# K projection of six token tiles as one level of Strassen over head pairs, its weight operands streamed from memory

## The chip, the cores and the metric

One Trainium2 chip, all 8 NeuronCores (two dies of four). Every core runs the same program on its own 2,048 tokens and recomputes keys and values for the 2,048 tokens ahead of them, so no core talks to another. The metric is the device time in microseconds of the slowest core for one execution of the whole layer.

## The reference, cut to what matters

One decoder layer: a combined projection, two groups of attention heads (group A dilated, group B a sliding window), `w_out`, LayerNorm, SwiGLU, LayerNorm. The change touches the projection of group A's keys and, lightly, the rotary tables of the queries.

```python
proj = jnp.einsum('bsd,de->bse', x, w_in) + b_in          # d = 2048
qa, ka, va, qb, kb, vb = jnp.split(proj, cuts, axis=-1)   # ka: 8 heads x 128
ka = rope(ka.reshape(B, S, 8, 128), pos)                  # [x1*cos - x2*sin, x2*cos + x1*sin]
...
qa = rope(qa.reshape(B, S, 8, 128), pos); qb, kb = rope(...)   # heads of 64 in group B
```

## The kernel before

The program has three phases: phase 1 projects K and V of all 4,096 tokens of a core, phase 2 projects the queries and does the attention, phase 3 does `w_out`, the norms and the feed-forward layer (itself in Strassen form, most of the span). The change lies in phase 1, with a small piece in phase 2.

Phase 1 holds the tokens as x tiles 0 to 7 of 512 tokens: `xs[slot]` is [128, 16 chunks of the contraction, 512 tokens], cast from float32 to bf16 by the load. Tiles 0 and 1 open the program (V by quarters of the contraction, while the weights still arrive). Then each tile t runs:

- two **V units** (`v_unit`, from tile 2 on), one level of Strassen over contraction halves, token halves and column halves: seven products "4 5 1 2 3 7 6" of eight matmuls, on four PSUM banks A, B, Dk, C. Products 1, 2, 5, 6, 7 read sums of x (`xp`, `xq`, `xr`) which `x_sum(t, 0..2)` makes on VectorE during the tile before. Product "7" adds into bank A and can start only when VectorE has read A into `v4`;
- from tile 3 on one **kb tile** and one **vb tile**, the small projections for group B;
- eight **K tiles** (`k_tile(t, h)`, h = head): 16 matmuls of 512 columns with the resident weights `wk[h]`, then the rotation `rope_a(..., swap=True)`: two ScalarE copies of 64 partitions that swap the halves, then three VectorE operations, then a store to `ka` in memory. `nx("bk", 8)` hands the eight PSUM banks out in turn.

The order of work is that in which the Python code calls the helpers; every engine runs its own instructions strictly in that order. `Sched` derives the semaphore waits from named buffers and byte ranges: a buffer laid over an older one waits for all the readers of the older one. A DMA is an instruction of its queue's engine: `"pool"` (needed for the casting loads), `"sp"` or `"act"`. The DMA waits for its buffers in that engine's order, so what is behind it in the queue waits too.

Phase 2 begins with `phase2_loads` in tile 7: three query weights on the pool queue (`wq`), the group B tables `rb` on the ScalarE queue. The group A tables `ra` come in one load of 2,048 KB in unit u = 3 of 32. `proj(tau)` is a query tile; tau 0 to 31 use `rb`, tau 32 to 63 use `ra`, and unit u runs `proj(u + 6)`.

The softmax here doesn't subtract the row's maximum and nothing guards it: scores larger than these inputs give would overflow.

## Time and profile before

| | us |
|---|---|
| median of 3 runs | 2787.43 |
| the runs | 2787.43, 3201.25, 2781.75 |
| profiled execution, span of the slowest core | 2774.6 |
| TensorE busy in it | 2720.6 |
| K projection units of tiles 2 to 7 (six of 27.6) | 166 |

The span runs from the first to the last instruction of the core. Of the profiled execution only this span is given; the two lower runs lie 7.2 and 12.8 us above it, which is what lies around a span. The run of 3201.25 us is disturbed and is left out of comparisons. Times inside the profile are counted from the span's start, and a stretch is named by them (tile 4's K units are 207.6 to 235.2).

### The profile page before, as it was taken

How to read it: one execution, taken by the hardware profiler on the slowest of the kernel's cores; microseconds unless marked ns; L12 is line 12 of the kernel's file. 1: busy time of each engine (PE TensorE's matmuls, PEld its weight loads, DVE VectorE, ACT ScalarE, POOL GpSimd, SP SyncE). 2: the span in 40 equal slices, each digit the busy share in tenths (PEclk: the TensorE clock that was granted, in tenths of full speed). 3: DMA queues.
4: the chain of work that ended last, by engine and by line, in shares of the span. 5: the costliest groups of instructions: out<-in, count | busy, mean ns of one | idle time of the engine just before them, and what ended most of it. 6: DMA issues, size and time to landing. Idle time of an engine off the chain costs nothing.

```text
span 2774.6 us, 41975 instructions; the slowest of 8 cores (2770.5 to 2774.6 us)
## 1 busy us (share of the span) xinstructions
PE 2720.6 (98%) x14991; PEld 1297.4 (47%) x14991; DVE 1990.6 (72%) x2758; ACT 843.0 (30%) x1229; POOL 569.9 (21%) x588
## 2 busy tenths in 40 slices
PE   8999999999999999999999999999999999999995
PEld 3444444445666444444444444444444444444442
DVE  4866665898888736788866666666988765766767
ACT  0312222787667237333200122111333100212115
POOL 3100000232112557311100101056000000000165
PEclk9999999999999999999999999999999999999998
DMA  9953135567567648789989776788799798555734
GB/s 153 193 118 87 48 86 134 114 130 150 129 149 188 198 144 250 124 154 157 149 169 211 135 122 114 129 227 212 164 171 167 144 194 188 85 83 90 174 115 122
DMA packets 254159, 407.23 MB, mean 147 GB/s; under 512 B 91969, under 2 KB 129985, under 8 KB 253378
## 3 DMA queue, kind: packets, MB, share of 16 engines
q0 software_dynamic: 92336, 193.64, 44.7%
q1 hardware_dynamic: 146066, 179.44, 21.7%
q10 hardware_dynamic: 15552, 31.46, 3.5%
q8 instruction: 122, 2.00, 0.3%
q14 instruction: 83, 0.68, 0.1%
HBM read 490.84 MB, written 104.27 MB: 214 GB/s over the span
## 4 chain that ended last, share of the span: by engine, by line
PE 91%; DMA 3%; DVE 3%; issue 1%; ACT 1%; POOL 0%; DVEq 0%; ACTq 0%; POOLq 0%; SPq 0%
PE sp L1570 57%; PE sp L902 8%; PE sp L1376 8%; PE sp L640 6%; PE sp L576 5%; DMA arena<-xT 3%; PE sp L1094 1%; PE sp L522 1%; PE sp L1112 1%; PE sp L945 1%; PE sp L971 1%; PE sp L620 1%; PE sp L661 1%; PE sp L1036 1%; PE sp L987 0%
## 5 line engine op out<-in xcount | busy, mean ns | idle before, releaser
L1570 PE MATMUL sp<-arena 128*128 128x512 f16 x7408 | 1600.0, 379 | 0.0
L1570 PEld LDWEIGHTS sp<-arena 128*128 128x128 f16 (+1 forms) x7408 | 724.7, 98 | 875.7 <-issue 3.1
L1844 DVE TENSOR_TENSOR arena<-sp,arena 128x512 f32<-128x512 f32 (+1 forms) x348 | 236.6, 689 | 161.0 <-PE sp L1570 141.9
L1930 DVE TENSOR_TENSOR arena<-arena,sp 128x512 f32<-128x512 f32 x257 | 169.9, 683 | 147.5 <-PE sp L1570 147.2
L902 PE MATMUL sp<-arena 128*128 128x512 bf16 x1024 | 236.8, 379 | 3.0 <-DVE arena L356 3.0
L140 POOL DMA_DIRECT2D arena<-wup x88 | 66.7, 758 | 771.8 <-DVE arena L1583 461.3
L1376 PE MATMUL sp<-arena 128*128 128x512 bf16 x1024 | 221.8, 379 | 2.2 <-DVE arena L1365 2.2
L640 PE MATMUL sp<-arena 128*128 128x512 bf16 x1024 | 222.2, 379 | 0.0
L1878 ACT ACTIVATE arena<-sp 128x512 f32<-128x512 f32 x86 | 51.4, 597 | 416.9 <-PE sp L1570 416.9
L363 ACT ACTIVATE arena<-sp,arena 64x512 f32<-64x512 f32 x136 | 92.9, 683 | 273.1 <-PE sp L640 247.4
L1419 POOL TENSOR_TENSOR arena<-arena 128x512 f32<-128x512 f32 x117 | 149.4, 1278 | 112.9 <-DVE arena L1930 74.0
L1418 ACT ACTIVATE arena<-arena 128x512 f32<-128x512 f32 x117 | 73.7, 630 | 283.3 <-DVE arena L1930 136.7
L1591 DVE TENSOR_TENSOR arena<-arena 128x2048 f16<-128x2048 bf16 (+1 forms) x118 | 159.4, 1351 | 0.0
L1376 PEld LDWEIGHTS sp<-arena 128*128 128x128 bf16 x1024 | 100.1, 98 | 124.2 <-issue 4.6
L1583 DVE TENSOR_TENSOR arena<-arena 128x2048 f16<-128x2048 bf16 (+1 forms) x118 | 157.3, 1333 | 0.0
L640 PEld LDWEIGHTS sp<-arena 128*128 128x128 bf16 x1024 | 100.0, 98 | 119.7
L1844 DVE TENSOR_TENSOR arena<-arena 128x512 f16<-128x512 f32 (+1 forms) x304 | 154.9, 568 | 0.3 <-issue 0.3
L1421 POOL TENSOR_TENSOR arena<-arena 128x512 f32<-128x512 f32 x117 | 151.1, 1292 | 9.2 <-ACT arena L1418 8.2
L902 PEld LDWEIGHTS sp<-arena 128*128 128x128 bf16 x1024 | 95.5, 98 | 120.7 <-issue 12.2
L576 PE MATMUL sp<-arena 128*128 128x512 f16 (+1 forms) x672 | 147.9, 379 | 1.6 <-DVE arena L586 1.6
L1841 ACT ACTIVATE arena<-sp 128x512 f32<-128x512 f32 x90 | 53.5, 597 | 277.8 <-PE sp L1570 248.8
L1053 ACT ACTIVATE arena<-sp 128x1024 bf16<-128x1024 f32 x96 | 97.4, 1020 | 68.2 <-PE sp L1047 56.4
(153 smaller groups left out, 2602.3 us busy)
## 6 DMA issues: line engine op xcount, KB each, us to landing
arena<-wup POOLq DMA_DIRECT2D x88, 1024.0 KB, 11.3
arena<-wdn POOLq DMA_DIRECT2D x22, 1408.0 KB, 16.5
z2s<-arena SPq DMA_DIRECT2D x39, 512.0 KB, 12.8
arena<-wob SPq DMA_DIRECT2D x32, 512.0 KB, 4.9
arena<-xres SPq DMA_DIRECT2D x32, 512.0 KB, 5.9
x1s<-arena ACTq DMA_DIRECT2D x64, 256.0 KB, 5.3
arena<-z2s SPq DMA_DIRECT2D x29, 512.0 KB, 12.3
arena<-wdb POOLq DMA_DIRECT2D x10, 1408.0 KB, 11.0
```

The costliest lines, as they stand in the source:

```text
L576: ins = nc.tensor.matmul(bank(k, bk), w[:, c, :], m[:, c, :], start=(first and c == 0), stop=(last and c == 7), skip_group_check=True)
L640: ins = nc.tensor.matmul(bank(k, bk), wk[h][:, kc, :], x[:, kc, :], start=(kc == 0), stop=(kc == KC - 1))
L902: ins = nc.tensor.matmul(bank(k, bk), w[:, kc, :], x[:, kc, :], start=(kc == 0), stop=(kc == KC - 1))
L1053: S_.act(lambda: nc.scalar.activation(out=p, in_=sp[:, :], func=AF.Exp, scale=scA), spb[s], [bp])
L1376: ins = nc.tensor.matmul(bank(k, bk), w[:, kc, :], y[:, kc, hh * 512:(hh + 1) * 512], start=(first and i == 0), stop=(last and i == len(kc ...
L1419: S_.pool(lambda: nc.gpsimd.tensor_tensor(out=za, in0=za, in1=z, op=ALU.add), [bz, bza], [bza])
L1421: ss["pend"] = [lambda: S_.pool(lambda: nc.gpsimd.tensor_tensor(out=qa, in0=qa, in1=sq, op=ALU.add), [bsq, bqa], [bqa])]
L1570: ins = nc.tensor.matmul(bank(k, bk), w, x, start=(first and i == 0), stop=(last and i == len(ws) - 1), skip_group_check=True)
L1583: S_.dve(lambda: nc.vector.tensor_tensor(out=v, in0=w[:, 0:n, :], in1=w[:, n:2 * n, :], op=ALU.add), [bw], [b])
L1591: S_.dve(lambda: nc.vector.tensor_tensor(out=v, in0=w[:, :, 0:128], in1=w[:, :, 128:256], op=ALU.subtract), [bw], [b])
L1844: S_.dve(lambda: nc.vector.tensor_tensor(out=o, in0=a, in1=b, op=op), [ba, bb], [bo])
L1930: S_.dve(lambda: nc.vector.tensor_tensor(out=v, in0=v, in1=o, op=op), [b, bo], [b])
```

## The change

For x tiles 2 to 7 the eight `k_tile`s are replaced by four `k_pair(t, p, mids)`. A pair takes heads 2p and 2p+1, the two halves of the contraction and the two 256-token halves, and forms the four output blocks from seven products of eight matmuls of 256 columns: 224 matmuls a tile where there were 128 of 512 columns. Its moving operands are the x sums that the V units already have. Its stationary operands are seven blocks for each pair, five of them sums of weights:

- `k_sums(p)` makes them on VectorE: three sums into a scratch of three buffers `kg`, two in place in `wk`. Seven stores of 256 KB on SyncE's queue put all seven into a new array `kwc` in memory. Pairs 0 to 2 are done inside tile 1 (behind `k_tile(1, 3)`, `(1, 5)`, `(1, 7)`), pair 3 behind the first V unit of tile 2.
- `k_load(t, p)` brings the seven blocks back, in two DMAs (1,024 and 768 KB) on the pool queue, into one of two places over the old `wk`. Pair p of a tile ends with the load for the pair after the next.

The results of the products are combined by two or three ScalarE copies and five VectorE operations of 256 columns a pair, and the rotation then works from memory-side float32 tiles (`ca`, `cb`): per head the two half copies on ScalarE and three VectorE operations of 512 columns. The rotations of a pair run inside the next pair (`mids`); those of pair 3 run inside the first V unit of the next tile (`settled`). The three x sums for the next tile all move to pair 3. The vb tile moves ahead of the V units, `load_x`, `load_ta` and `load_tb` to the new places. In phase 2 `rb` becomes four buffers and moves onto what was `wv`/`wkb`, and `ra` is loaded over it in four pieces behind units 23 to 26.

```diff
+    k.kwc_d = dt("kwc", [4, 128, 7, 1024], BF16, kind="Internal").ap()
...
+    OPS = "4512376"
...
+    def k_sums(p):
+        blk = lambda h, i: wk[h][:, 8 * i:8 * i + 8, :]
+        h0, h1 = 2 * p, 2 * p + 1
+        gs = []
+        for i, (a, b_, op) in enumerate((((h0, 1), (h0, 0), ALU.subtract), ((h0, 0), (h1, 1), ALU.add), ((h1, 0), (h1, 1), ALU.subtract))):
+            o_ = o_kg + 2048 * i
+            v, b = view(k, o_, 1024, F16).rearrange("p (a b) -> p a b", a=8), S_.buf("kg%d_%d" % (p, i), o_, o_ + 2048)
+            S_.dve(lambda v=v, a=a, b_=b_, op=op: nc.vector.tensor_tensor(out=v, in0=blk(*a), in1=blk(*b_), op=op), [bwk[h0], bwk[h1]], [b])
+            gs.append((o_, b))
+        for d, o in (((h0, 1), (h1, 1)), ((h1, 0), (h0, 0))):
+            S_.dve(lambda d=d, o=o: nc.vector.tensor_tensor(out=blk(*d).bitcast(F16), in0=blk(*d), in1=blk(*o), op=ALU.add),
+                   [bwk[h0], bwk[h1]], [bwk[d[0]]])
+        src = {"4": gs[0], "1": gs[1], "3": gs[2], "2": (o_k + 4096 * h0, bwk[h0]), "7": (o_k + 4096 * h0 + 2048, bwk[h0]),
+               "6": (o_k + 4096 * h1, bwk[h1]), "5": (o_k + 4096 * h1 + 2048, bwk[h1])}
+        bw = []
+        for i, n in enumerate(OPS):
+            o_, b_ = src[n]
+            b = Buf("kwc%d_%d" % (p, i))
+            S_.dma("sp", k.kwc_d[p, :, i, :], view(k, o_, 1024), [b_], [b], "kwc")
+            bw.append(b)
+        k.bkwc[p] = bw
+
+    def k_load(t, p):
+        if t > 7:
+            return
+        o_ = o_k + 4096 + 14336 * (p % 2)
+        for a, e in ((0, 4), (4, 7)):
+            b = S_.buf("kw%d_%d_%d" % (t, p, a), o_ + 2048 * a, o_ + 2048 * e)
+            S_.dma("pool", view(k, o_ + 2048 * a, 1024 * (e - a)), k.kwc_d[p, :, a:e, :].rearrange("p a n -> p (a n)"), k.bkwc[p][a:e], [b], "kw")
+            for i in range(a, e):
+                v = view(k, o_ + 2048 * i, 1024, BF16 if OPS[i] in "25" else F16).rearrange("p (a b) -> p a b", a=8)
+                KW[t, p, OPS[i]] = (v, b)
...
+    def k_pair(t, p, mids):
...
+        A, B, Dk, C = [nx("bk", 8) for _ in range(4)]
+        lo, up = slice(0, 256), slice(256, 512)
+        W = {"4": (x[:, 8:16, up], bxt), "3": (x[:, 0:8, lo], bxt), "1": (xq3, [bxq]), "5": (xp3[:, :, lo], [bxp]),
+             "2": (xp3[:, :, up], [bxp]), "7": (xr3[:, 8:16], [bxr]), "6": (xr3[:, 0:8], [bxr])}
+
+        def prod(n, bk, first, last):
+            (w, bw), (m, bm) = KW[t, p, n], W[n]
...
+            def mm():
+                for c in range(8):
+                    ins = nc.tensor.matmul(bank(k, bk)[:, 0:256], w[:, c, :], m[:, c, :], start=(first and c == 0), stop=(last and c == 7),
+                                           skip_group_check=True)
+                return ins
+            S_.pe(mm, [bw] + bm, [k.bBK[bk]])
...
+        prod("4", A, True, True)
+        S_.act(lambda: nc.scalar.activation(out=v4, in_=ps[A], func=AF.Identity, bias=bias(h0), scale=1.0), [bb[A], k.bsmall], [b4])
+        mid()
+        prod("5", B, True, True)
+        S_.act(lambda: nc.scalar.activation(out=v5, in_=ps[B], func=AF.Copy), [bb[B]], [b5])
+        prod("1", Dk, True, True)
+        S_.dve(lambda: nc.vector.tensor_tensor(out=v5, in0=ps[Dk], in1=v5, op=ALU.subtract), [bb[Dk], b5], [b5])
+        prod("2", C, True, True)
+        S_.dve(lambda: nc.vector.tensor_tensor(out=ca[:, up], in0=ps[C], in1=v4, op=ALU.add), [bb[C], b4], [bca])
+        mid()
+        prod("3", B, False, True)
+        S_.act(lambda: nc.scalar.activation(out=cb[:, lo], in_=ps[B], func=AF.Identity, bias=bias(h1), scale=1.0), [bb[B], k.bsmall], [bcb])
+        prod("7", A, False, True)
+        S_.dve(lambda: nc.vector.scalar_tensor_tensor(out=ca[:, lo], in0=ps[A], scalar=bias(h0), in1=v5, op0=ALU.add, op1=ALU.add),
+               [bb[A], b5, k.bsmall], [], [bca])
+        prod("6", C, False, True)
+        k_load(t if p < 2 else t + 1, (p + 2) % 4)
+        S_.dve(lambda: nc.vector.tensor_tensor(out=v5, in0=v5, in1=ps[C], op=ALU.subtract), [bb[C], b5], [b5])
+        S_.dve(lambda: nc.vector.scalar_tensor_tensor(out=cb[:, up], in0=ps[B], scalar=bias(h1), in1=v5, op0=ALU.add, op1=ALU.add),
+               [bb[B], b5, k.bsmall], [], [bcb])
+        mid()
...
+        def rope(h, c, bc):
...
+            for i, j in ((0, 64), (64, 0)):
+                S_.act(lambda i=i, j=j: nc.scalar.activation(out=t2[i:i + 64], in_=c[j:j + 64], func=AF.Copy), [bc], [bt2] if i == 0 else [],
+                       [bt2] if i else [])
+            ko, bko = KO[ki := nx("ko", 5 if t < 6 else 3)]
+            S_.dve(lambda: nc.vector.tensor_tensor(out=c, in0=c, in1=ra[:, 0, :], op=ALU.mult), [bc, bra], [bc])
+            S_.dve(lambda: nc.vector.tensor_tensor(out=t2, in0=t2, in1=ra[:, 1, :], op=ALU.mult), [bt2, bra], [bt2])
+            S_.dve(lambda: nc.vector.tensor_tensor(out=ko, in0=c, in1=t2, op=ALU.add), [bc, bt2], [bko])
...
+        return [lambda: rope(h0, ca, bca), lambda: rope(h1, cb, bcb)]
...
+    for h in range(8):
+        k_tile(1, h)
+        if h in (2, 4, 6):
+            x_sum(2, h // 2 - 1)
+        if h in (3, 5, 7):
+            k_sums(h // 2 - 1)
+    k_temps()
+    k_load(2, 0)
+    load_x(4, (8, 8))
+    load_ta(3)
...
+    def settled(t):
+        while ropes:
+            ropes.pop(0)()
...
+        if t == 5:
+            load_x(7, (8, 8))
...
+    for t in range(2, 8):
+        if t >= 3:
+            vb_tile(t)
+        v_unit(t, 0, lambda: settled(t - 1))
+        if t == 2:
+            k_sums(3)
+            k_load(2, 1)
+        if t >= 3:
+            kb_tile(t)
...
-        for h in range(8):
-            k_tile(t, h)
-            xi = {2: 0, 4: 1, 6: 2} if t == 1 else {1: 0, 3: 1, 5: 2}
-            if h in xi and t < 7:
-                x_sum(t + 1, xi[h])
...
+        for p in range(4):
+            mids = ropes + [lambda: None] * (2 - len(ropes))
+            if p == 3 and t < 7:
+                r = mids.pop(1)
+                mids += [lambda: (x_sum(t + 1, 0), x_sum(t + 1, 1)), lambda: (x_sum(t + 1, 2), r())]
+            ropes = k_pair(t, p, mids)
+            if t == 7 and p == 1:
                 phase2_late(k)
...
+    k.o_ra = P.o
+    k.rb = [P("rb%d" % t, 1024, F32) for t in range(4)]
...
     for t in range(4):
-        S_.dma("act", k.rb[:, t], k.ropeB_d[t], [], [], "rbq", joins=[k.brb])
+        S_.dma("act", k.rb[t][0], k.ropeB_d[t], [], [k.rb[t][1]], "rbq")
...
-        S_.dma("sp", ra, k.ropeA_d[4:8].rearrange("t p a b -> p t a b"), [], [bra], "raq")
...
+    def load_ra(t):
+        o = o_ra + t * 4096
+        v, b = view(k, o, 1024, F32), S_.buf("raq%d" % t, o, o + 4096)
+        S_.dma("sp", v, k.ropeA_d[4 + t], [], [b], "raq")
+        ra.append((v.rearrange("p (a b) -> p a b", a=2), b))
...
+        if 23 <= u < 27:
+            load_ra(u - 23)
```

Where the instructions stand now, at three places.

VectorE at the end of tile 1, from the rotation of `k_tile(1, 6)` to the first read of a V unit's bank A (L586 before, L589 after), before:

```order
L356 SCALAR_TENSOR_TENSOR arena<-sp,arena 128x512 [waits e_act]
L366 TENSOR_TENSOR arena<-arena 128x512
L359 TENSOR_TENSOR arena<-arena 128x512 [waits e_dve,d_56]
L556 TENSOR_TENSOR arena<-arena 128x4096 [waits d_52,d_51,d_5]
L356 SCALAR_TENSOR_TENSOR arena<-sp,arena 128x512 [waits e_act]
L366 TENSOR_TENSOR arena<-arena 128x512
L359 TENSOR_TENSOR arena<-arena 128x512 [waits e_dve,d_57]
L586 TENSOR_TENSOR arena<-sp,arena 128x512 [waits e_pe]
```

and after (L357/L367/L360 are the rotation, L559 is `x_sum`, L626 and L629 are `k_sums`):

```order
L357 SCALAR_TENSOR_TENSOR arena<-sp,arena 128x512 [waits e_act]
L367 TENSOR_TENSOR arena<-arena 128x512
L360 TENSOR_TENSOR arena<-arena 128x512 [waits e_dve,d_56]
L559 TENSOR_TENSOR arena<-arena 128x4096 [waits d_52,d_51,d_5]
L357 SCALAR_TENSOR_TENSOR arena<-sp,arena 128x512 [waits e_act]
L367 TENSOR_TENSOR arena<-arena 128x512
L360 TENSOR_TENSOR arena<-arena 128x512 [waits e_dve,d_57]
L626 TENSOR_TENSOR arena<-arena 128x1024 [waits d_2]
L626 TENSOR_TENSOR arena<-arena 128x1024 [waits d_60]
L626 TENSOR_TENSOR arena<-arena 128x1024 [waits d_64]
L629 TENSOR_TENSOR arena<-arena 128x1024 [waits e_dve] x2
L589 TENSOR_TENSOR arena<-sp,arena 128x512 [waits e_pe]
```

The five weight sums of pair 2 now stand ahead of the V unit's first read; those of pairs 0 and 1 stand likewise behind heads 3 and 5. The waits `d_...` of L626 are for stores that still read `kg`.

The pool queue from the load of x tile 3 on, before:

```order
L140 DMA arena<-xT 128x8x512 [waits e_pe]
L140 DMA arena<-xT 128x8x512
L140 DMA arena<-xT 128x8x512 [waits e_pe]
L140 DMA arena<-xT 128x8x512 [waits d_53,d_52,d_51,d_5,d_4,d_3,d_2,d_1,d_0]
```

and after (128x4096 and 128x3072 are the two parts of a `k_load`; the first two x rows are tile 3, the next two tile 4):

```order
L140 DMA arena<-xT 128x8x512 [waits e_pe]
L140 DMA arena<-xT 128x8x512
L140 DMA arena<-kwc 128x4096 [waits d_65,d_63,d_62,d_54,d_3]
L140 DMA arena<-kwc 128x3072 [waits d_64,d_2,d_66,d_4,d_61]
L140 DMA arena<-xT 128x8x512
L140 DMA arena<-xT 128x8x512 [waits d_1,d_0]
L140 DMA arena<-kwc 128x4096 [waits d_71,d_69,d_67,d_52]
L140 DMA arena<-kwc 128x3072 [waits d_72,d_57]
L140 DMA arena<-kwc 128x4096 [waits e_pe]
```

The load of tile 4 now stands behind `k_load(2, 0)`, whose waits `d_...` are stores of `kwc`, and `k_load(2, 1)` stands behind the load of tile 4.

SyncE's queue in the first half of phase 2, before:

```order
L140 DMA ys<-arena 128x2048 [waits e_dve]
L140 DMA arena<-ropeA 128x4x1024
L140 DMA ys<-arena 128x2048 [waits e_dve] x4
L140 DMA arena<-ka 128x8x512 [waits d_56,d_0,d_5]
L140 DMA arena<-vs 128x17x128
L140 DMA arena<-vs 128x5x128 x4
L140 DMA arena<-vs 128x16x128 x2
```

and after:

```order
L140 DMA ys<-arena 128x2048 [waits e_dve] x5
L140 DMA arena<-ka 128x8x512 [waits d_50,d_58,d_1]
L140 DMA arena<-vs 128x17x128
L140 DMA arena<-vs 128x5x128 x4
L140 DMA arena<-vs 128x16x128 x2
L140 DMA ys<-arena 128x2048 [waits e_dve]
L140 DMA arena<-ropeA 128x1024 [waits e_dve] x4
L140 DMA ys<-arena 128x2048 [waits e_dve] x2
```

The tables `ra` moved from ahead of the loads of head 0's keys and values (`ka`, `vs`) to behind them.

## Rows read from the trace of the kernel before

**Rows 1.** The page, parts 1 and 4: busy time, chain that ended last.
```profile
PE 2720.6 (98%) x14991; PEld 1297.4 (47%) x14991; DVE 1990.6 (72%) x2758; ACT 843.0 (30%) x1229; POOL 569.9 (21%) x588
...
PE 91%; DMA 3%; DVE 3%; issue 1%; ACT 1%; POOL 0%; DVEq 0%; ACTq 0%; POOLq 0%; SPq 0%
PE sp L1570 57%; PE sp L902 8%; PE sp L1376 8%; PE sp L640 6%; PE sp L576 5%; DMA arena<-xT 3%; PE sp L1094 1%; PE sp L522 1%; PE sp L1112 1%; PE sp L945 1%; PE sp L971 1%; PE sp L620 1%; PE sp L661 1%; PE sp L1036 1%; PE sp L987 0%
```

**Rows 2.** Spans and clock: die 1, whose median core is the longer.
```profile
die 1 (median of its cores): 2772.5 us, clock 0.996
```

**Rows 3.** TensorE timeline: start us, us, line, shape, count, idle before.
```profile
127.83 8.80 PE L576 MATMUL sp<-arena 128*128 128x512 f16 x40
137.71 13.97 PE L576 MATMUL sp<-arena 128*128 128x512 f16 x64 [1.09 <-DVE arena L586]
...
207.60 27.79 PE L640 MATMUL sp<-arena 128*128 128x512 bf16 x128
...
263.07 3.74 PE L620 MATMUL sp<-arena 128*128 128x128 bf16 x64
```

**Rows 4.** Windows of tile 4's K units and of tile 5's V/kb/vb units.
```profile
207.60:235.20 27.60, 27.60 (x131) 12.53 (x129) 20.02 (x27) 9.56 (x14) 0.00 (x0) 1.00 0.12 40
235.20:266.60 31.40, 31.40 (x194) 16.15 (x193) 17.57 (x26) 3.25 (x5) 1.75 (x2) 1.00 0.72 140
```

**Rows 5.** VectorE timeline at the end of tile 1.
```profile
120.71 2.29 DVE L556 TENSOR_TENSOR arena<-arena 128x4096 f16<-128x4096 bf16 x1 [4.80 <-DMA arena<-xT]
122.92 0.74 DVE L356 SCALAR_TENSOR_TENSOR arena<-sp,arena 128x512 f32<-128x512 f32 x1
...
125.04 0.74 DVE L356 SCALAR_TENSOR_TENSOR arena<-sp,arena 128x512 f32<-128x512 f32 x1
...
127.17 1.22 DVE L556 TENSOR_TENSOR arena<-arena 128x2048 f16<-128x2048 bf16 x1
...
136.88 1.28 DVE L586 TENSOR_TENSOR arena<-sp,arena 128x512 f32<-128x512 f32 x2
```

**Rows 6.** VectorE timeline, a 128-wide operation on PSUM.
```profile
196.69 0.29 DVE L392 TENSOR_TENSOR arena<-sp,arena 128x128 f32<-128x128 f32 x1 [0.26 <-PE sp L389]
```

**Rows 7.** ScalarE timeline, the half copies of one K unit.
```profile
157.73 1.38 ACT L363 ACTIVATE arena<-sp,arena 64x512 f32<-64x512 f32 x2 [12.20 <-PE sp L640]
```

**Rows 8.** DMA issues of 60 to 77 us: KB each, us to landing.
```profile
vs<-arena SPq DMA_DIRECT2D x8, 256.0 KB, 19.5
```

**Rows 9.** DMA issues of 300 to 360 us.
```profile
arena<-xT POOLq DMA_DIRECT2D x2, 1024.0 KB, 18.3
vs<-arena SPq DMA_DIRECT2D x4, 256.0 KB, 2.1
```

**Rows 10.** Windows: PEclk, DMA share of 16 engines and GB/s stand last.
```profile
120.00:140.00 20.00, 18.91 (x89) 8.45 (x87) 18.43 (x24) 4.70 (x7) 1.76 (x2) 1.00 1.14 178
140.00:156.00 16.00, 15.45 (x73) 6.88 (x71) 7.97 (x13) 0.60 (x1) 0.00 (x0) 1.00 0.98 192
...
443.80:450.00 6.20, 6.20 (x32) 2.81 (x30) 1.66 (x3) 1.36 (x2) 2.69 (x5) 1.00 1.04 328
```

**Rows 11.** DMA issues of 440 to 465 us.
```profile
arena<-wq POOLq DMA_DIRECT2D x3, 512.0 KB, 14.1
```

**Rows 12.** DMA issues of the whole span.
```profile
arena<-wdb POOLq DMA_DIRECT2D x10, 1408.0 KB, 11.0
```

**Rows 13.** SyncE queue timeline: issuing DMAs.
```profile
600.93 26.58 SPq L140 DMA_DIRECT2D arena<-vs  x7
627.61 14.58 SPq L140 DMA_DIRECT2D ys<-arena  x2
```

**Rows 14.** VectorE timeline: first rotation of a group-A query tile.
```profile
643.93 0.75 DVE L356 SCALAR_TENSOR_TENSOR arena<-sp,arena 128x512 f32<-128x512 f32 x1
```

**Rows 15.** Window at the end of the span, TensorE idle: clock.
```profile
5.00:10.00 5.00, 1.98 (x5) 0.80 (x4) 0.00 (x0) 2.28 (x4) 5.00 (x10) 1.00 1.02 139
2765.00:2770.00 5.00, 0.00 (x0) 0.00 (x0) 1.30 (x3) 3.56 (x5) 0.00 (x0) 0.50 1.07 320
```

65 lines of the change are left out of this document (38 added, 27 removed).

## The prediction

> **What bounds the kernel now.** I read the page first: TensorE is busy 98% of the span and carries 91% of the chain that ended last; K tiles (L640) are 6% of it [rows 1]. The clock is full: die 1's mean is 0.996 [rows 2]. In phase 1 the TensorE timeline is nearly without gaps, so removed matmul time reaches the end if nothing else takes its place. The one idle piece at this place is telling: 1.09 us at 137.7 in the first V unit of tile 2, waiting for VectorE [rows 3]. Next the windows: in a K stretch of 27.6 us VectorE is busy 20.0, DMA 12%; in the V stretch behind it VectorE 17.6 of 31.4 [rows 4]. But up to 156 us the 16 DMA engines are full (share 1.14, then 0.98) [rows 10], and VectorE sat 4.80 us before the first x sum of tile 2, which came at 120.71 instead of some 116 [rows 5]. So phase 1 has slack in the middle and none at the start of tile 2.
>
> **Products.** A K stretch has 128 matmuls in 27.79 us; less the drained last one (379 ns) that is 215.8 ns each. 64 matmuls of 128 columns with a weight load each take 3.74 us, less 219 ns: 55.9 ns each [rows 3]. At 256 columns the line through both gives 109.2 ns (no row has 256 columns alone); loads pass at 55.9, so they do not bind. 224 x 109.2 = 24.5 us for 27.6: 3.15 us off a tile, **-18.9 us** for six. Bounds: 224 x 107.9 (half of 215.8), -20.6 us; 224 x 111.8 (twice 55.9), -15.6.
>
> The Trainium skill speaks against this: TensorE: Matmul & The Clock Gate, Back-to-back issue gap, gives 81 ns for a matmul of 128 columns and 131 for one of 512 in a stream with weight loads. A line through those is 98 at 256; by it a K stretch would be 16.8 us before and 21.9 after, 5 us slower. The rows have 215.8 and 55.9, so the measurement decides.
>
> **VectorE inside the K stretch.** An operation of 512 columns is busy 0.69, one of 128 columns 0.29 [rows 6]; 256 lies at 0.42. A rotation takes 2.12 us of VectorE (122.92 to 125.04) [rows 5], and still has three operations of 512. A pair has two rotations and five operations of 256: 2 x 2.1 + 5 x 0.42, with some 0.2 for each dependent step, about 6.7 us, for 6.1 us of matmuls. In addition a rotation waits for two ScalarE half copies (1.38 us together [rows 7]) which start only when `ca` is finished. Product "6" of pair p waits for the operation that reads bank C, and this stands behind a rotation of pair p-1. Following one tile: pair 0 has no rotation and waits for nothing; "6" of pair 1 is due at 11.3 and may go at 11.9; pair 2 loses 0.7, pair 3 0.75. The stretch is 26.4, not 24.4: +2.0 a tile. In tile 2 load waits (below) cover it; five tiles, **+10 us**. Bounds: 0 (the busy sum fits in the stretch) and +16 (pairs 1 to 3 wholly at VectorE's 7.2).
>
> **VectorE behind the K stretch.** From that bank read (25.4) VectorE has three x sums (2.29 + 1.22 + 2.29 [rows 5]), three operations of pair 3, and three rotations before it reads bank A of the next V unit: 25.4 + 5.7 + 1.3 + 0.6 (vb) + 6.4 = 39.4, done at 39.9. Product "7" is due 5 products of 1.73 behind the vb tile: 26.4 + 3.6 + 8.65 = 38.65. Lost: 1.2 us a tile; in tile 3 (vb 1.0 instead of 3.6) somewhat more, but its backlog is less after tile 2. Five times, **+6 us** (0 to 12). The x sums can't hide elsewhere: x sums of tile t+1 overwrite what pair 3 reads last.
>
> **Weight sums in tile 1.** Fifteen operations of 1,024 columns. 4,096 columns take 2.29 and 2,048 1.22, so 1,024 about 0.6, with two dependent steps 3.1 us for a pair. The chain from 120.71 to 136.88 has no gap and ends in the read of bank A that TensorE already waits for [rows 3, 5]. So 9.3 us go on the path whole; that is the floor. Above it: each sum into `kg` waits for the stores of the pair before. Eight stores of just this size took 19.5 us to land beside the casting loads [rows 8], against 2.1 us for one alone [rows 9]. The fifth of seven then lands some 14 us after its issue at 126 to 128, while pair 1's sums are due at 134: 6 us; pair 2 finds the ring still full: 2 to 5 more, eased when tile 3's load ends. I take 8: **+17 us** (9 to 24) at the first "7" of tile 2.
>
> **First loads of tile 2.** `k_load(2, 1)` needs: pair 3's stores (behind the first V unit), and the pool queue, where tile 4's load stands ahead of it, itself behind `k_load(2, 0)` with its waits for pair 2's stores. Tile 4's load takes 18.3 us with free engines [rows 9]. By the times above: pair 2's stores landed 160, tile 4's load issued 161.5 and landed about 183, the first part of `k_load(2, 1)` 187. The best rate in view is 328 GB/s [rows 10] and I use some 300: 1,024 KB is 3.5 us. TensorE reaches pair 1 at 170.5 + 6.1 = 176.6 and waits **+10.5 us** (5 to 20). As a check the work of the full engines: rest of tile 3's load 16, 28 stores 25 (at some 300 GB/s), tile 4's load 16, two `k_load`s 10, other stores 7, from 120.7: 195 at the latest, so 187 is not too late.
>
> **Steady loads.** `k_load(t, 2)` is issued 3.7 us into the stretch (its part for "7" and "6" at 6.2) and needed at 12.2; four parts, 3.67 MB, must land within 16 us: 225 GB/s. At 300 GB/s they do, at no cost. But 1,408 KB from `wdb`, same kind and queue, landed in 11.0 us in the median [rows 12], 131 GB/s with its fixed part: below the need (a rival).
>
> The Trainium skill (DMA: Bandwidth & Descriptors, Anatomy of one DMA) fits 2.0 us + bytes / 436 GB/s: 4.4 us for 1,024 KB. By an estimate from it the queue of tile 2 would clear at about 170 and the +10.5 would be 0. Its figures are for a transfer by itself; the row has 19.5 us for 256 KB, so I keep the rows.
>
> **Tile 7.** `phase2_loads` puts three `wq` loads on the pool queue ahead of `k_load(7, 2)`. They landed in 14.1 us in the median, beside 2 MB on the ScalarE queue [rows 11]; the third about 18 us into the stretch. Then 3.5 us: 21.7, needed at 12.8: **+9 us** (4 to 13).
>
> **Phase 2.** SyncE spent 26.58 us issuing head 0's value loads (from 600.93) [rows 13]; `ra` now comes behind them, issued from 628 and landing about 640 behind small packets. The first rotation that needs it ran about 640 (the one at 643.93 is the second [rows 14]). VectorE may wait: **+3 us** (0 to 8). The moves of `rb`, of the tables and of `vb` I put at nothing: same bytes, in stretches with 12% DMA.
>
> **Clock.** TensorE never rested 10 us in the middle of the before. At the end, idle, its granted clock is 0.50, and 1.00 in 5 to 10 us with 3 us of rest [rows 15]. Three rests of about 10 us could each end at the 1.2 GHz level for a few us: **+3 us** (0 to 8).
>
> **Sum.** -18.9 + 10 + 6 + 17 + 10.5 + 9 + 3 + 3 = +39.6 us on a span of 2774.6: 2814 us. The median lies 12.8 above this span, so 2787.4 + 39.6 = **2827 us**, 1.4% slower. A measurement of this kernel tells about 2% from no change, that is 2731.7 and 2843.2.
>
> **Rivals.** (1) **The covers hold**: loads in time, stores fast, VectorE catches up. What stays is -18.9 and the floor of 9.3, 2778 us; if even this vanishes (tile 2's x lands earlier), 2768.5. For it: DMA 12% busy and VectorE 27% idle in a K stretch [rows 4]; against it: full engines until 156 us. (2) **The stream binds every tile**, the one that ends beyond my forecast: at `wdb`'s 131 GB/s the four parts need 28 us from 3.7, 33 with the fixed part, where "3" of pair 3 is due at 23: 10 us a tile in place of the 2 of VectorE, five tiles, +40: 2867 us. It decides from the point where the rate in a K stretch is under 225 GB/s; above, it costs nothing. Against it: 328 GB/s [rows 10]. (3) **The page's matmul spacing**: six times +5 instead of -3.15, 2876 us; the rows leave it no chance to speak of. (4) **A store-bound start**: the `kwc` traffic stretches all of tiles 2 and 3, +30 beyond the forecast.
>
> **Chances.** Forecast's case 0.52 (2800 to 2850), rival 1 0.23, rival 2 0.17, rival 4 0.07, rival 3 0.01. The range that leaves out about 2 in 10 goes from 2768 (rival 1 at its best) to 2867 (rival 2). Faster by over 2% would need 56 us, three times all that the products give: 0.01. Slower by over 2%: rivals 2, 3 and 4, and a twelfth of the forecast's case: 0.29. The same: 0.70.
>
> **What the profile after would show.** Products: eight matmuls of 256 columns in about 0.87 us; a tile of 224 without waits in 24.5. VectorE: short waits of TensorE before "6" (bank C) in pairs 1 to 3, and at the first "7" of each V unit from tile 3 on. Weight sums: a TensorE wait of 10 to 25 us in the first V unit of tile 2, VectorE itself waiting for `kwc` stores. Loads: a TensorE wait of 5 to 20 us for `kwc` in pair 1 of tile 2, one of 4 to 13 us in pair 2 of tile 7, none in tiles 3 to 6. Phase 2: VectorE waiting for `ropeA`. I am wrong if the loads of tiles 3 to 6 land in over 12 us, if the engines drain so fast that `kg` is free in time, or if TensorE's stretch in tiles 4 to 6 is 24.5 or above 27.6.

## The result, and the profile after

The changed kernel took 2849.38 and 2879.72 us, against 2781.75 to 2787.43 us for the kernel before in the same comparison: a ratio of 1.0286, 95% interval [1.0191, 1.0381]. It is slower, by an amount whose interval contains the 2% mark. The profiled execution took 2849.38 us; by the medians of die 1 in the two profiles (2831.8 for 2772.5 us) the change is 2.1% slower. In some executions, here and in the experiments, one die or both had a lower granted clock (die 1 of the 2879.72 us run had 0.97); I leave the clearly longer ones out of the ratios, and where no others exist I read the cores of the other die, or waits alone, and give no ratio.

The page of the kernel after, parts 1 and 4, as in [rows 1], and the median of die 1, as in [rows 2]:

```profile
PE 2733.6 (96%) x15567; PEld 1355.0 (48%) x15567; DVE 2043.9 (72%) x2898; ACT 869.2 (31%) x1301; POOL 592.9 (21%) x636
...
PE 83%; DVE 5%; DMA 5%; issue 3%; ACT 2%; SPq 1%; POOL 0%; DVEq 0%; ACTq 0%; POOLq 0%
PE sp L1702 55%; PE sp L1508 8%; PE sp L1032 7%; PE sp L579 3%; PE sp L671 2%; DMA arena<-xT 2%; SPq L140 1%; PE sp L525 1%; PE sp L1224 1%; DMA kwc<-arena 1%; DMA arena<-kwc 1%; ACT arena L708 1%; DVE arena L559 1%; PE sp L1242 1%; PE sp L768 1%
```

```profile
die 1 (median of its cores): 2831.8 us, clock 0.987
```

TensorE is busier in microseconds than before, though the products have fewer columns, and its share of the chain fell from 91 to 83%; `kwc` transfers in both directions now stand in the chain. Die 1 is 59.3 us longer than before. Die 0 (median 2844.1 us, clock 0.983), with the slowest core (core 2, clock 0.980), had further dips of the clock, so I account on core 5 of die 1: 2771.9 us before, 2835.1 after, +63.2.

TensorE's timeline on core 5, before (marks at the start of the K stretches of tiles 2, 3 and 6 and of phase 2):

```profile
151.93 27.79 PE L640 MATMUL sp<-arena 128*128 128x512 bf16 x128
...
205.57 27.79 PE L640 MATMUL sp<-arena 128*128 128x512 bf16 x128
...
382.69 27.79 PE L640 MATMUL sp<-arena 128*128 128x512 bf16 x128
...
469.36 5.99 PE L902 MATMUL sp<-arena 128*128 128x512 bf16 x27
```

The same after, with every wait of over 1 us in tiles 2 to 4 and 7:

```profile
146.10 3.57 PE L579 MATMUL sp<-arena 128*128 128x512 f16 x8 [10.93 <-ACT arena L595]
153.73 17.13 PE L579 MATMUL sp<-arena 128*128 128x512 f16 x72 [4.07 <-DVE arena L589]
170.70 6.28 PE L671 MATMUL sp<-arena 128*128 128x256 bf16 x56
198.78 14.35 PE L671 MATMUL sp<-arena 128*128 128x256 bf16 x104 [21.80 <-DMA arena<-kwc]
...
232.56 8.29 PE L579 MATMUL sp<-arena 128*128 128x512 f16 x24 [3.30 <-ACT arena L595]
...
253.73 11.57 PE L671 MATMUL sp<-arena 128*128 128x256 bf16 x104
...
292.06 5.59 PE L579 MATMUL sp<-arena 128*128 128x512 f16 x24 [1.02 <-ACT arena L595]
...
313.25 11.57 PE L671 MATMUL sp<-arena 128*128 128x256 bf16 x104
...
471.00 5.59 PE L579 MATMUL sp<-arena 128*128 128x512 f16 x24 [1.37 <-ACT arena L595]
...
515.13 7.89 PE L671 MATMUL sp<-arena 128*128 128x256 bf16 x56 [9.00 <-DMA arena<-kwc]
524.40 5.46 PE L671 MATMUL sp<-arena 128*128 128x256 bf16 x48 [1.39 <-DMA arena<-kwc]
...
532.93 7.07 PE L1032 MATMUL sp<-arena 128*128 128x512 bf16 x32 [1.54 <-DVE arena L695]
```

The K stretch of tile 2 starts 18.8 us late (170.70 for 151.93). From there to the K stretch of tile 3 it is 83.0 us for 53.6: +29.4. A steady tile takes 59.52 (253.73 to 313.25) for 59.04 (a third of 205.57 to 382.69): +0.5. From the K stretch of tile 6 (432.30 after) to phase 2 it is 100.6 for 86.7: +14.0. With three steady periods that is 18.8 + 29.4 + 1.4 + 14.0 = 63.6 us at the start of phase 2, and 63.2 at the end: on this core phases 2 and 3 add nothing, and the whole loss is in phase 1, three quarters of it in the start of the scheme. The start of phase 2 on die 1 was 469.2 us in the median of its cores before, 527.6 after; I use that number below.

The window of 128 to 200 us on core 5 after (the busy times of TensorE, its weight loads, VectorE, ScalarE and GpSimd; PEclk, DMA share and GB/s last). Before, TensorE was busy for 71.5 us of it, VectorE for 48.2, and the DMA share was 0.72:

```profile
128.00:200.00 72.00, 35.20 (x175) 17.64 (x174) 34.98 (x53) 5.25 (x9) 5.02 (x8) 0.77 0.97 241
```

TensorE is busy for half of it, VectorE less than before, and the 16 DMA engines all the time; the clock fell to 0.77 in the mean. What these engines did shows in the DMA issues of 160 to 205 us (KB each, us to landing), and in the pool queue's issue of the first part of `k_load(2, 1)`:

```profile
arena<-xT POOLq DMA_DIRECT2D x2, 1024.0 KB, 25.3
arena<-kwc POOLq DMA_DIRECT2D x2, 1024.0 KB, 17.1
kwc<-arena SPq DMA_DIRECT2D x7, 256.0 KB, 12.2
```
```profile
182.10 0.56 POOL L140 DMA_DIRECT2D arena<-kwc  x1 [15.73 <-DMA kwc<-arena]
```

The load that pair 1 waits for could be issued only when a store of `kwc` had landed, at 182.1, and then took 16.7 us.

In a steady tile VectorE isn't full. In its K stretch it is busy for 19.7 of 26.7 us, about the share that it had before (20.0 of 27.6 in [rows 4]), and yet TensorE waits for it:

```profile
253.70:280.40 26.70, 25.24 (x225) 21.48 (x224) 19.66 (x36) 12.87 (x24) 3.74 (x7) 1.00 0.77 250
```

In the V stretch behind it VectorE's work grew, from 17.6 us ([rows 4]) to 23.4.

### The profile page after: what moved, and what is told of

Its sections match the earlier page's. It is cut to its first block, busy times and chain, and to the rows that moved or that the text cites. A ratio compares the mean times of both kernels' runs of the same rounds, so it can differ in the third digit from the quotient of the medians.

```text
span 2848.3 us, 43824 instructions; the slowest of 8 cores (2825.4 to 2848.3 us)
## 1 busy us (share of the span) xinstructions
PE 2733.6 (96%) x15567; PEld 1355.0 (48%) x15567; DVE 2043.9 (72%) x2898; ACT 869.2 (31%) x1301; POOL 592.9 (21%) x636
## 4 chain that ended last, share of the span: by engine, by line
PE 83%; DVE 5%; DMA 5%; issue 3%; ACT 2%; SPq 1%; POOL 0%; DVEq 0%; ACTq 0%; POOLq 0%
PE sp L1702 55%; PE sp L1508 8%; PE sp L1032 7%; PE sp L579 3%; PE sp L671 2%; DMA arena<-xT 2%; SPq L140 1%; PE sp L525 1%; PE sp L1224 1%; DMA kwc<-arena 1%; DMA arena<-kwc 1%; ACT arena L708 1%; DVE arena L559 1%; PE sp L1242 1%; PE sp L768 1%
## 5 line engine op out<-in xcount | busy, mean ns | idle before, releaser
L1702 PEld LDWEIGHTS sp<-arena 128*128 128x128 f16 (+1 forms) x7408 | 725.4, 98 | 887.0 <-issue 36.9
L1032 PE MATMUL sp<-arena 128*128 128x512 bf16 x1024 | 239.9, 383 | 8.2 <-DVE arena L357 6.7
L1508 PE MATMUL sp<-arena 128*128 128x512 bf16 x1024 | 223.4, 381 | 1.4 <-DVE arena L1497 1.4
L671 PE MATMUL sp<-arena 128*128 128x256 f16 (+1 forms) x1344 | 156.3, 277 | 33.9 <-DMA arena<-kwc 25.6
L579 PE MATMUL sp<-arena 128*128 128x512 f16 (+1 forms) x672 | 155.9, 391 | 23.6 <-ACT arena L595 16.6
L1508 PEld LDWEIGHTS sp<-arena 128*128 128x128 bf16 x1024 | 100.3, 98 | 124.7 <-issue 5.6
L671 PEld LDWEIGHTS sp<-arena 128*128 128x128 f16 (+1 forms) x1344 | 130.9, 99 | 59.7 <-issue 39.1
L1032 PEld LDWEIGHTS sp<-arena 128*128 128x128 bf16 x1024 | 95.9, 98 | 128.6 <-issue 21.9
L579 PEld LDWEIGHTS sp<-arena 128*128 128x128 f16 (+1 forms) x672 | 66.0, 100 | 109.2 <-issue 37.4
## 6 DMA issues: line engine op xcount, KB each, us to landing
arena<-wdn POOLq DMA_DIRECT2D x22, 1408.0 KB, 16.7
```

Source lines behind the costliest of these rows:

```text
L579: ins = nc.tensor.matmul(bank(k, bk), w[:, c, :], m[:, c, :], start=(first and c == 0), stop=(last and c == 7), skip_group_check=True)
L671: ins = nc.tensor.matmul(bank(k, bk)[:, 0:256], w[:, c, :], m[:, c, :], start=(first and c == 0), stop=(last and c == 7), skip_group_check ...
L1032: ins = nc.tensor.matmul(bank(k, bk), w[:, kc, :], x[:, kc, :], start=(kc == 0), stop=(kc == KC - 1))
L1508: ins = nc.tensor.matmul(bank(k, bk), w[:, kc, :], y[:, kc, hh * 512:(hh + 1) * 512], start=(first and i == 0), stop=(last and i == len(kc ...
L1702: ins = nc.tensor.matmul(bank(k, bk), w, x, start=(first and i == 0), stop=(last and i == len(ws) - 1), skip_group_check=True)
```

## The experiments

**x4 behind tile 2 (e1).** Edit:

```
-    load_x(4, (8, 8))                      # after k_load(2, 0)
...
+        if t == 2:
+            load_x(4, (8, 8))              # after the pairs of tile 2
         if t < 4 and t > 1:
```

> The load of x tile 4 moves on the pool queue from between the two first weight loads of tile 2 to behind tile 2, beside that of x tile 5. If the wait before pair 1 of tile 2 (16.6 us on core 2, 21.8 on core 5) comes from the place in the queue, it falls to 0 to 6 us, the granted clock stays at 1.00 behind it, and the whole gets 17 to 25 us shorter than the changed kernel. Rival: the 16 DMA engines are simply full at this place, whatever the order; then the wait stays above 12 us and the whole changes by less than 6 us.

TensorE's timeline of this kernel on core 5, and its larger weight loads of 160 to 205 us:

```profile
184.60 14.31 PE L671 MATMUL sp<-arena 128*128 128x256 bf16 x104 [5.26 <-DMA arena<-kwc]
```
```profile
arena<-kwc POOLq DMA_DIRECT2D x5, 1024.0 KB, 6.8
```

The wait fell from 21.8 to 5.3 us, and these loads land in 6.8 us instead of 17.1. A wait of 1.74 us for weights is new in tile 3 (at 255.09), where x4 now lands. The first of them was issued at 177.7 us for 182.1, and both times its queue waited for a store of `kwc` and not for the place behind x4: what x4 takes is a share of the engines. Phase 2 starts at 515.1 us (median of die 1), 12.5 earlier. I compare starts of phase 2 here and not spans, because on this chip, which e2, e3 and e4 share, the kernel before took 2786.5 us on the same die (median of six executions) and not 2772.5. The wait is where it was expected and the gain is short of the 17 to 25 us. Core 5 had the longest wait of its die: in the median of die 1 it fell from 19.6 to 5.1, and some of that came back in tile 3 (0.9 and 1.7 us on two of the four cores). The two waits ahead were longer on core 5 (11.55 and 6.71), but not in the median of the die (15.3 us in sum for 15.1).

**Operands with their own scratch buffer stored first (e4).** Edit: the stores of a pair in the order 4, 1, 3, 5, 2, 7, 6.

```
-        for i, n in enumerate(OPS):
+        for i in (0, 2, 4, 1, 3, 5, 6):
```

> The seven stores of a pair's weight blocks go out in another order: the three from the scratch first. If VectorE's waits for these stores in tile 1 (0.77, 3.70, 3.19, 0.97, 1.42 us) delay the first V unit of tile 2, they fall to under 4 us together and the two waits of that unit (15.5 us on core 2) get 5 to 7 us shorter. Two theories for the whole: the terms add up, then it gets 5 to 7 us shorter; or the wait before pair 1 is set by the DMA queue's own clock time (its load landed at 193), then that wait grows by the same amount and the whole stays within 2 us.

The waits in the first V unit were 9.5, 0.8 and 4.8 us, 15.1 for 15.0, and the second 21.0 for 21.8; phase 2 started at 526.6, 1 us earlier. VectorE's own waits for these stores were 5.0 us for 6.6, where under 4 was expected. The order of the stores is worth nothing measurable; this expectation failed.

**Stores of one pair only (e8).** This run stores only pair 0, and loads pair 0's operands for every pair; it leaves out 21 of the 28 stores, and so the K of three pairs.

```
+            if p == 0:
                 S_.dma("sp", k.kwc_d[p, :, i, :], ..., "kwc")
```

> Only the seven operands of head pair 0 are stored to memory, and every load reads those; the sums on VectorE are all still made. It leaves out 21 of the 28 stores (5.25 MB) and so the K of three pairs. Theory (the transfers between 128 and 200 us hold the start): VectorE's waits for stores (6.6 us on core 5) go, the two waits in the first V unit (10.9 and 4.1 us) fall to 5 to 9 in sum, the second stall of 21.8 falls under 4, phase 1 ends 20 to 27 us earlier (506 to 513 on core 5 for 532.9) and the span is as much shorter. Rival (VectorE's own work for the sums holds the start): less than 8 us is gained.

The ratio to the kernel before was 1.0159 [1.0082, 1.0235]. TensorE's and VectorE's timelines on core 5:

```profile
145.57 3.57 PE L579 MATMUL sp<-arena 128*128 128x512 f16 x8 [11.32 <-ACT arena L595]
153.20 16.39 PE L579 MATMUL sp<-arena 128*128 128x512 f16 x64 [4.07 <-DVE arena L589]
172.06 3.42 PE L579 MATMUL sp<-arena 128*128 128x512 f16 x8 [2.46 <-DVE arena L589]
175.32 11.57 PE L672 MATMUL sp<-arena 128*128 128x256 bf16 x104
```
```profile
131.93 0.69 DVE L626 TENSOR_TENSOR arena<-arena 128x1024 f16<-128x1024 bf16 x1 [1.24 <-DMA kwc<-arena]
135.81 0.69 DVE L626 TENSOR_TENSOR arena<-arena 128x1024 f16<-128x1024 bf16 x1 [3.19 <-DMA kwc<-arena]
140.32 0.69 DVE L626 TENSOR_TENSOR arena<-arena 128x1024 f16<-128x1024 bf16 x1 [3.82 <-DMA kwc<-arena]
```

The second wait is gone on core 5 (21.8 to 0), 4.6 and 2.4 us are left of it on cores 3 and 7, and under 0.7 on the others; phase 2 starts at 509.5, 18.1 us earlier. But the waits in the first V unit did not fall: 17.9 us for 15.0 on core 5, 12.1 to 17.9 on the eight cores for 13.4 to 17.0. That part of my theory was wrong, and the second view shows why: the three scratch buffers are shared by the pairs, and pair 1's sums wait 8.3 us for pair 0's stores, which are still there. So the two stalls have different causes. The first is VectorE's chain: fifteen sums in its order, and its wait for pair 0's stores. I read this from the timeline, where from the first sum on the chain runs without another gap of over 0.2 us up to the read that TensorE waits for; no run leaves the sums themselves out. The second is the bytes.

**Weight sums on GpSimd (e7).** The three sums of each pair that go to the scratch buffers are made by GpSimd (and stored first).

```
-            S_.dve(lambda ...: nc.vector.tensor_tensor(out=v, ...), [bwk[h0], bwk[h1]], [b])
+            S_.pool(lambda ...: nc.gpsimd.tensor_tensor(out=v, ...), [bwk[h0], bwk[h1]], [b])
```

> The three of five weight sums of each head pair that go to the scratch buffers are computed by GpSimd (12 operations of 128x1024, 0.69 us each on VectorE), and stored first. Theory (two causes at the start: VectorE's order in tiles 1 and 2, and transfers that are too many between 128 and 200 us): VectorE's waits for stores (6.6 us in sum) and 8.3 us of its work go, so the two waits in the first V unit (10.9 and 4.1 us on core 5) fall to 7 or less in sum; but the weight loads of pair 1 land no earlier than before (198 us), so that the second stall grows by what the first gives, and the span stays within 4 us of 2832. Rival (VectorE's order alone holds the start): pair 1 lands earlier by as much, and the span is 8 to 15 us shorter. GpSimd's 1.28 us for 128x512 in float32 gives 2.6 us for each of these, 31 us in all, which lies beside 55 us.

TensorE's clock on core 5 was 0.89 in the mean, here and in e5 (described below), which ran on the same chip with the start unchanged, so I compare the waits of these two. On core 5 those of the first V unit were 6.2, 7.1 and 4.0 us, 17.3 in sum: not under 7, and twice the 8.2 of e5. On every core they grew by 8 to 12 us. The wait before pair 1 fell (6.5 us for 19.9), because TensorE came later: pair 1 started at 196.3 for 199.3 on core 5, but 4.4 us later in the median of the eight cores. So the loads of pair 1 landed no earlier, as expected, and VectorE was not freed. Its timeline shows why, beside GpSimd's:

```profile
105.33 7.84 DVE L367 TENSOR_TENSOR arena<-arena 128x512 f32<-128x512 f32 x1
...
143.07 1.49 DVE L629 TENSOR_TENSOR arena<-arena 128x1024 f16<-128x1024 bf16 x2 [9.44 <-POOL arena L626]
```
```profile
106.31 6.30 POOL L626 TENSOR_TENSOR arena<-arena 128x1024 f16<-128x1024 bf16 x3
```

An operation of 0.68 us took 7.84, and ended 0.6 us after GpSimd's third. On each of the eight cores one VectorE operation beside these three took 5.0 to 7.8 us and ended 0.6 us after them. What matters more for the start is the second line: the two sums that VectorE makes in place overwrite what GpSimd still has to read, so VectorE waited 9.4 us (8.6 to 11.5 on the eight cores) for GpSimd, which itself had waited for pair 0's stores.

**wq behind the weight loads (e2).** Edit: the three `wq` loads move from `phase2_loads` to `phase2_late`, behind `k_load(7, 3)`.

> The three loads of query weights in tile 7 move from ahead of the last two weight loads to behind them. If these stand in the queue, the wait before pair 2 of tile 7 (8.3 us on core 2, 9.0 on core 5, and 0.8 to 1.4 before its product 3) falls to under 2 us and with the clock that stays up the whole gets 9 to 14 us shorter. Rival: at this place a weight load is slow by itself (group B's tables load at the same time on another queue); then at least 5 us of wait stay.

TensorE, VectorE and the DMA issues on core 5:

```profile
527.73 8.67 PE L1032 MATMUL sp<-arena 128*128 128x512 bf16 x32 [11.93 <-DVE arena L695]
```
```profile
526.38 0.69 DVE L713 TENSOR_TENSOR arena<-arena 128x512 bf16<-128x512 f32 x1 [10.56 <-DMA ka<-arena]
```
```profile
arena<-kwc POOLq DMA_DIRECT2D x2, 1024.0 KB, 8.1
...
arena<-vs SPq DMA_DIRECT2D x1, 544.0 KB, 21.2
```

The weight loads of tile 7 land in 8.1 us (20.2 in the change as given, where the `wq` loads stand in front), and no product of tile 7 waits for them. But phase 2 starts at 527.0, only 0.6 us earlier, where 9 to 14 were expected: the wait is now at its first product. VectorE may not overwrite a K buffer until its `ka` store has landed, and that store stood on SyncE's queue behind the load of `vB`, 544 KB in small packets, 21.2 us.

**The boundary as a whole (e5).** As e2, and `vB` and the two masks move to the start of `phase2`, behind the last `ka` stores.

> The three wq loads stand behind the last weight load of tile 7, and the vB load and the two masks leave the middle of tile 7 for the start of phase 2, behind the last ka stores. Moving wq alone only moved the wait: the weight loads then took 8.1 and 8.6 us and not 20, but the store of a K tile waited behind vB on SyncE's queue and VectorE for it (10.56 us), so that TensorE stood 11.9 us at its first product of phase 2. Theory (one place in the queues is enough: the transfers around tile 7 fit if vB stands behind the stores): tile 7 has no wait over 2 us, the first product of phase 2 waits under 3 us, phase 1 of core 5 ends at 520 to 525 (532.9 in the change as given) and the span of an undisturbed die is 8 to 12 us shorter (2820 to 2824). Rival (the bytes are too many wherever they stand): vB lands after 548, the first attention of phase 2 waits for it, and the span stays within 3 us of 2832.

On core 5 no product of tile 7 waited for weights, and the first product of phase 2 waited 2.8 us; on the seven others the latter was 1.2 to 5.8, with 0.8 to 1.3 us in tile 7 on four of them. So 10.4 us of waits became 1 to 7. The span can't be judged here; c8 below has the same edit at full clock, where the first product waited 5.2 to 7.8 us.

**No rotation multiplications (e3).** This run leaves out two of the three VectorE operations of each rotation in the changed tiles, so K isn't rotated.

```
-            S_.dve(... out=c, in0=c, in1=ra[:, 0, :], op=ALU.mult ...)
-            S_.dve(... out=t2, in0=t2, in1=ra[:, 1, :], op=ALU.mult ...)
```

> Leaves out the two multiplications by cosine and sine in the rotation of tiles 2 to 7 (the copies and the last addition stay). If VectorE's order gives back the gain of the products, the waits before product 6 (0.57 + 0.50 + 0.50 us a tile) and the one in the next V unit (1.02 us) go, a K stretch falls from 26.7 to 24.6 us, the period of tiles 4 to 6 from 59.5 to 56.5, and the whole gets 13 to 20 us shorter. Rival: the stretch is long because 224 matmuls of 256 columns are slower than the line through the other widths says; then it stays above 26.

TensorE on core 5:

```profile
239.30 24.87 PE L671 MATMUL sp<-arena 128*128 128x256 bf16 x224
264.01 3.74 PE L725 MATMUL sp<-arena 128*128 128x128 bf16 x64
...
296.13 24.78 PE L671 MATMUL sp<-arena 128*128 128x256 bf16 x224
...
352.16 24.79 PE L671 MATMUL sp<-arena 128*128 128x256 bf16 x224
```

All 224 products of a K stretch run without a gap in 24.7 us (239.30 to 264.01), for 26.7 with the rotations and 27.6 before. The first period is 56.8 us and the next 56.0 (296.13 to 352.16): there the V stretch is back at the 31.4 us of the kernel before, and the tile gains the whole 3.0 us that the products give. Phase 2 starts at 505.3, 22.3 us earlier. So in the K stretch the rotations take back two thirds of what the products give, and in the V stretch the rest and more.

**No stream (e9).** The operands are loaded in tile 2 only, and tiles 3 to 7 use what lies in the buffers, so 40 of 48 weight loads are left out, and K is another.

```
         if t > 7:
             return
+        if t > 2:
+            for n in OPS:
+                KW[t, p, n] = KW[2, 2 + p % 2, n]
+            return
```

> The operands are loaded in tile 2 alone; tiles 3 to 7 use what lies in the two buffers (pairs 2 and 3 for all). It leaves out 40 of the 48 weight loads (35 MB) and so gives another K. Theory (the stream is hidden in tiles 3 to 6 and VectorE sets their K stretch): K stretch 26.7 and period 59.5 as in the change as given, waits of 0.50 to 0.57 on VectorE's L690 unchanged; in tile 7 the waits of 9.0 and 1.4 us for weights go, span 9 to 13 us shorter. Rival (the stream slows the products or takes the clock): the K stretch falls under 26 and the period under 58.7, span 15 us shorter or more.

The ratio was 1.0187 [1.0123, 1.025]. TensorE on core 5:

```profile
322.89 6.27 PE L675 MATMUL sp<-arena 128*128 128x256 f16 x56 [0.63 <-DVE arena L694]
...
382.42 6.27 PE L675 MATMUL sp<-arena 128*128 128x256 f16 x56 [0.63 <-DVE arena L694]
```

The period is 59.53 us for 59.52 and the waits for VectorE are the same, though the DMA share of 320 to 380 us fell from about 0.5 to 0.16. The stream costs nothing in tiles 3 to 6: my second rival is excluded for them. Tile 7's waits for weights went, and the spans of both dies (median 2824.7) are some 7 us shorter than in the change as given, where 9 to 13 were expected; smaller waits for ScalarE (2.5 and 0.9 us) took the place of the rest.

**The third x sum later (e6).** Edit: `x_sum(t + 1, 2)` moves from the last pair's `mids` to behind product "2" of the next V unit.

> The third sum over x (2.28 us on VectorE) is written behind product 2 of the first V unit of the next tile, and no more ahead of the rotations that the last pair leaves. Theory (VectorE's backlog at the end of the K stretch, handed on by ScalarE's copy of product 5, is what holds the V stretch): the wait of 1.02 us at that copy goes, the one of 3.30 in tile 3 falls to about 1, the V stretch is 31.8 us, the period 58.5 for 59.52, the span 5 to 8 us shorter (2824 to 2827 on an undisturbed die). Rival (the sum is only moved to where product 7 needs it): a wait of 1 us or more appears there, and the span stays within 2 us of 2832.

The wait at ScalarE's copy went, and one of 1.5 us for this sum came at product "7" (DVE L559, 287.00 in tile 4) in every tile, 3.0 in tile 3: the rival was right as to the waits, VectorE's backlog has to be paid once. The span can't be judged (clock 0.90).

**All five at once (c5).** e1, e4, e5, e6 and e7 in one kernel, on the chip of e5, e6 and e7.

> All the repairs together: x4 behind tile 2, weight sums to the scratch buffers on GpSimd and stored first, the third x sum late, wq, vB and the masks behind. If the terms are separate, they add up: about 11 for x4 (measured on core 5), 8 to 12 for the boundary to phase 2, 5 to 8 for the sum, 0 to 8 for the start, so a span of 2795 to 2808 on an undisturbed die for 2832 of the change as given and 2772.5 of the kernel before; the rest of the loss against before is then the start of tile 2. Rival (each repair only moves the wait to the next transfer): 2815 or more.

No product of pair 1 of tile 2 waited for weights, but the first V unit waited 7.4, 7.2 and 3.4 us, product "7" of each tile 1.3 to 1.5, and the first product of phase 2 3.8 on core 5. With TensorE's clock at 0.90 to 0.94 in these tiles the span can't be compared, and the sum is open; the waits show that two of the five (e6, e7) gave nothing. What was expected of the sum of the five stays untested.

**Three places in the queues (c8).** e1, e4 and e5 together: nothing is computed otherwise than in the change.

> The change with three places in the queues altered and nothing computed otherwise: x4 behind tile 2, the scratch operands of a pair stored first, and wq, vB and the masks behind the last weight load and the last ka stores. The terms measured so far on an undisturbed die or as waits: about 11 for x4, 0 to 2 for the order of the stores, 5 to 8 for the boundary (a wait of 2 to 6 us is left at the first product of phase 2). Theory: span 2810 to 2817 for 2831.8, ratio to the kernel before 1.014 to 1.017; what is left against the kernel before is the start of the scheme in tile 2. Rival (the repairs take from each other): 2820 or more.

Three runs took 2820.38 to 2825.60 us, ratio 1.0149 [1.0074, 1.0225]. TensorE on core 5:

```profile
141.21 3.57 PE L579 MATMUL sp<-arena 128*128 128x512 f16 x8 [7.20 <-ACT arena L595]
153.80 18.32 PE L579 MATMUL sp<-arena 128*128 128x512 f16 x72 [9.02 <-DVE arena L589]
...
183.19 13.20 PE L671 MATMUL sp<-arena 128*128 128x256 bf16 x104 [4.96 <-DMA arena<-kwc]
...
510.80 8.69 PE L1033 MATMUL sp<-arena 128*128 128x512 bf16 x32 [5.64 <-DVE arena L695]
```

Phase 2 starts at 510.4, 17.2 us earlier, and the span is 2814.3 for 2831.8 (median of die 1, and of all nine dies at full clock), within what was expected. The edits add up: 12.5 of x4 and some 5 of the boundary. What is left is 42 us against the kernel before. On core 5 it is made of 16.2 us of waits behind VectorE's chain in the first V unit of tile 2, 5.0 for pair 1, 5.6 at the start of phase 2, 3.3 and 2.1 in tile 3, and half a microsecond in each steady tile, besides what the clock takes after such rests.

**Half of the rotations on GpSimd (c7).** As c8, with the three operations of the odd heads' rotations on GpSimd, and `k_load` on SyncE's queue.

```
+            on, e = (S_.pool, nc.gpsimd) if h % 2 else (S_.dve, nc.vector)
```

> As the kernel with three places altered, and the rotation of the odd heads (two multiplications and the sum, 128x512 in float32) on GpSimd, the weight loads therefore on SyncE's queue. Theory (VectorE sets the K stretch, 6.2 us of work and its handshakes for each pair beside 6.2 of products): the waits of 0.50 at L690 go, K stretch 24.7 for 26.7, V stretch 31.5 for 32.8 (fewer rotations ahead of ScalarE's copy), period 56 to 57, span 2795 to 2802. GpSimd's 1.28 us for 128x512 in float32 gives 3.9 us a pair beside 6.2. Rival (GpSimd stops VectorE while it works: in the run with weight sums on GpSimd one operation of VectorE took 7.84 us for 0.68 beside three of GpSimd's): K stretch 27 or more, span 2815 or more. Second rival: loads behind ka stores on SyncE come late and the K stretch shows waits for kwc.

The ratio was 1.0219 [1.0156, 1.0282], 20.7 us more than c8 (2835.0 for 2814.3, medians of the dies at full clock). TensorE's timeline and one line of VectorE's, then VectorE's and GpSimd's groups from 250 to 480 us, core 5 (count, busy us, mean ns):

```profile
364.28 11.58 PE L671 MATMUL sp<-arena 128*128 128x256 bf16 x104
...
385.10 5.46 PE L671 MATMUL sp<-arena 128*128 128x256 bf16 x48 [0.80 <-DMA arena<-kwc]
...
405.92 7.03 PE L579 MATMUL sp<-arena 128*128 128x512 f16 x24 [3.35 <-ACT arena L595]
...
428.54 11.57 PE L671 MATMUL sp<-arena 128*128 128x256 bf16 x104
```
```profile
373.45 0.69 DVE L712 TENSOR_TENSOR arena<-arena 128x512 f32<-128x512 f32 x1 [1.65 <-ACT arena L708]
```
```profile
L559 DVE TENSOR_TENSOR arena<-arena 128x4096 f16<-128x4096 bf16 x8 | 22.2, 2770 | 0.0
...
L713 DVE TENSOR_TENSOR arena<-arena 128x512 f32<-128x512 f32 x15 | 14.5, 968 | 0.0
```
```profile
L712 POOL TENSOR_TENSOR arena<-arena 128x512 f32<-128x512 f32 x15 | 27.4, 1828 | 135.0 <-ACT arena L708 135.0
```

The period is 64.3 us instead of 59.5. Both rivals came true: VectorE's x sums take 2.77 us for 2.28, its multiplications 0.97 for 0.68 and GpSimd's own 1.83, and the loads behind `ka` stores come 0.5 to 1.3 us late in each of the later pairs. ScalarE's copy is waited for 3.35 us instead of 1.02. The K stretch is 27.65 us for 26.67, with the late loads in it, and the V stretch 36.6 for 32.85: 2.3 of this is the longer wait at ScalarE's copy, and 1.4 is the slower clock behind it. How much of that wait comes from VectorE's slower operations and how much from the late loads the run doesn't tell.

What the theory promised didn't come either: the waits of 0.57 and 0.50 us at L690 are all there, though VectorE is busy for only 15.9 us of this K stretch (19.7 without the edit). L690 is the read of bank C, and ahead of it in VectorE's order stands the rotation of the even head, which stayed on VectorE and starts only when ScalarE has copied the halves (the line above: VectorE idle for 1.65 us, waiting for the copy). It starts 9.2 us into the stretch in pair 1 and 16.0 in pair 2, here as in the change as given. So what holds product "6" is this chain of dependent steps and not the amount of VectorE's work. The run without the multiplications (e3) shortened the chain and the work at once and could not tell the two apart.

## Why the prediction was nearly right, and where it was not

The forecast was 2827 us, slower by 1.4%; the profiled execution took 2849.4, and the kernel was slower by 2.9% (2.1% by the medians of die 1). The direction was right, the size too small: on core 5 the sum of +39.6 stands against +63.2 measured. The final number lay nearer than the sum by luck. I had added 12.8 us to the span for what lies around it, and in the profiled execution only 1.1 us lay there (2849.4 for a slowest core of 2848.3): the 7.2 and 12.8 us that I took for it before were differences between executions. The span itself was missed by 34 us (2848 for 2814). Term by term, on core 5:

| term | predicted | measured |
|---|---|---|
| products, per tile | -3.15 | -2.9 (24.7 for 27.6, e3) |
| VectorE in the K stretch, per tile | +2.0 | +1.96 (26.67 for 24.71) |
| VectorE behind it, per tile | +1.2 | +1.45 (32.85 for 31.4), 1.02 of it one wait |
| weight sums, first V unit of tile 2 | +17 | 15.0 (14.6 to 17.0 on die 1, from 13.4 on the chip) |
| first loads, pair 1 of tile 2 | +10.5 | 21.8 (15.1 to 21.8) |
| tile 7 behind wq | +9 | 10.4 |
| `ra` in phase 2 | +3 | VectorE waits 1.4, nothing at the end |
| clock | +3 | some 10 |

**Right.** The steady tile, by which the change was to gain, was predicted to within 0.5 us: 224 products of 256 columns at 110 ns, and a K stretch held by VectorE at 26.4, measured 26.67. e3 shows that the rotations are the cause, e9 excludes the stream, and c7 shows which part of my reasoning carried: the place of the read of bank C behind a rotation that waits for ScalarE, and not the busy sum of 6.7 us a pair. The weight sums cost what the chain of [rows 5] said, with VectorE's waits for `kwc` stores in it (6.0 us on core 5, estimated at 8). Tile 7's wait came where it was placed, and e2 shows that `wq` in front made it. What the prediction didn't see is that moving `wq` alone gives nothing, since SyncE's queue and the same engines are next.

**Right in size, wrong in place.** I looked for the loss behind the K stretch at product "7". It came at product "3", through ScalarE's copy of product "5" (L595): this writes the buffer that the last pair's rotation still reads, so it waits for VectorE, and TensorE for it. I had followed only VectorE's own reads of the banks. In tile 2 the wait at the same place, behind the last rotation of tile 1, was 10.93 us, followed by 4.07 at the place that I named.

**The step that was mis-sized** is "First loads of tile 2". It took tile 4's load at the 18.3 us of [rows 9], from a stretch where it ran alone, and the weight loads behind it at 300 GB/s, 3.5 us. They took 25.3 and 17.1 us, and cost a wait of 21.8 us for my 10.5: the stores, the x load and the weight loads shared the 16 engines, and each took longer than in the rows. The check in the same paragraph ("195 at the latest") came near, and I set it aside for the smaller number: pair 1 started at 198.8. That it came so near is in part luck, since it was made at 300 GB/s and the engines moved 241. e1 (5.3 us once x4 is away) and e8 (0 once 21 of the stores are) show both halves of it on core 5: it takes both to fill the engines.

**The clock.** Adding up what the pieces behind the rests took beyond the full clock (3.57 for 1.89; 17.13 for 15.7; 14.35 for 11.57; 8.29 for 5.59; 7.89 for 6.33) gives 10.2 us for my 3. I had priced three rests of 10 us; the engine rested five times there, for 10.9, 4.1, 21.8, 3.3 and 9.0 us, and on this core each piece of work behind one was slow.

**The fate of the rivals.** The covers did not hold (1). The stream binds none of the tiles 3 to 6 (2), by e9. The spacing that the Trainium skill gives (TensorE: Matmul & The Clock Gate, Back-to-back issue gap) (3) is refuted by e3: 110 ns for 256 columns. A store-bound start (4) came in part: 11 of its 30 us without the clock, in tile 2 and not in all of tiles 2 and 3.

**Small slips in the sums.** The upper bounds of two terms were off: "twice 55.9" gives some -15.4 us and not -15.6, and the "7.2" of VectorE behind the +16 stands in no row (the sum beside it is 6.7). Neither enters the forecast.

## What to carry to other kernels

Saved products are worth only what the other engines leave of them: 2.9 us a tile of TensorE became 0.9 in the K stretch, and a loss of 0.5 over the tile. A share of free time doesn't tell this: VectorE is idle for a quarter of the K stretch with and without the change. What counts is how long the chain of dependent steps is in front of the one read that frees a bank, and whether work that was pushed behind the stretch is done when the next engine needs it. Moving part of that work to another engine (c7) helps only if it stands in that chain. A scheme that prepares operands pays at its start, and there the transfers already under way decide: add up all bytes that must pass in the window and believe that number over the latency of one load by itself. And a load that is moved out of the way lands in front of somebody: follow the wait to the next queue before counting the gain.

## What the runs showed of the hardware

**VectorE and GpSimd slow each other.** In e7 a float32 operation of VectorE with both inputs in the arena took 7.84 us for 0.68 while GpSimd made three sums of bf16; in c7 VectorE's sums grew from 2.28 to 2.77 us in the mean, and GpSimd's from 1.26 (its shortest there) to 1.83. The Trainium skill (SBUF — State Buffer, Who interferes with whom) says that a `tensor_tensor` of VectorE with both inputs in SBUF contends with a GpSimd instruction that reads SBUF; both runs agree with it, and the 7.84 us show that VectorE can be held by three operations in a row. Which of the two was issued first the trace doesn't show: VectorE's record begins 1 us before GpSimd's first on core 5 and 1.9 us after it on core 1.

**The clock after a rest.** TensorE's granted clock was 0.50 in windows of 5 us inside the rests of core 5 (140 to 145, 185 to 200), that is 1.2 GHz, 0.56 from 200 to 205, with the engine at work again since 198.8, and 0.68 and 0.64 in the two windows from 230 to 240, in and behind a rest of 3.3 us. A short rest alone doesn't decide it: behind the same 3.3 us the same 24 products took 7.03, 8.29, 7.03 and 5.59 us on cores 4 to 7, and 5.60 on core 5 in e9.

**Load in company.** The same 1,024 KB of `kwc` landed in 17.1 us beside the load of x4 and the last stores, in 6.8 without x4 (e1, the same window of 160 to 205 us).
